# Residual stream kept token by feature: row-wise norms, turned tiles, token-wise output projections, and other lanes' blocks ahead of the steps of x's norms

## The reference, cut to what matters

```python
h = rms_norm(x, g_pre)            # over the 1024 features of a token
x = x + rms_norm(mix_or_ffn(h), g_post)
```

```python
(silu(h @ w_gate) * (h @ w_up)) @ w_down
```

## Time and profile before

| | |
|---|---|
| median of 3 runs | 2696.52 us (2694.02 to 2698.24) |
| the profiled execution | 2697.63 us |
| its span, first to last instruction | 2695.9 us |
| TensorE (PE) busy | 2507.8 us, 93% |
| VectorE (DVE) busy | 1706.4 us, 63% |
| ScalarE (ACT) busy | 1242.5 us, 46% |
| granted TensorE clock, mean | 0.969 |
| DMA read | 471.48 MB, 175 GB/s |

### The profile page before, as it was taken

The page is one execution under the profiler, slowest core; times in us unless marked ns, Lnnn a source line. Parts: engine busy times, 40 slices in busy tenths (PEclk is TensorE's granted clock), DMA queues, the critical chain, the costliest instruction groups (busy, mean ns, idle before and its releaser), DMA issues.

```text
span 2695.9 us, 48269 instructions
## 1 busy us (share of the span) xinstructions
PE 2507.8 (93%) x20500; PEld 2368.0 (88%) x20500; DVE 1706.4 (63%) x2804; ACT 1242.5 (46%) x1687; POOL 1.2 (0%) x6
## 2 busy tenths in 40 slices
PE   5799997899999999999998999999999999787998
PEld 5689996788998898999797999999999999766997
DVE  5565565456766656566777667577575558656655
ACT  4443352344545445455455544464444345444443
POOL 0000000000000000000000000000000000000000
PEclk9899998899999999999898999999999999898999
DMA  5456655623555665544362344455545555363453
GB/s 213 180 194 255 240 198 223 246 104 119 188 186 206 232 252 188 176 152 159 118 202 80 122 157 172 170 189 174 187 171 177 185 173 187 118 235 125 172 180 117
DMA packets 71588, 480.09 MB, mean 178 GB/s; under 512 B 8784, under 2 KB 9296, under 8 KB 17744
## 3 DMA queue, kind: packets, MB, share of 16 engines
q1 hardware_dynamic: 66240, 468.74, 48.9%
q10 hardware_dynamic: 5136, 8.28, 1.0%
HBM read 471.48 MB, written 1.05 MB: 175 GB/s over the span
## 4 chain that ended last, share of the span: by engine, by line
PE 75%; DVE 12%; ACT 6%; DMA 4%; issue 3%; ACTq 0%; DVEq 0%
PE bank L265 65%; ACT whi L224 3%; DMA raw<-w_main 2%; DVE wlo L244 2%; PE bank L302 2%; PE bank L1163 2%; DVE wlo L231 2%; PE bank L1045 1%; DMA raw<-w_down 1%; PE bank L983 1%; DVE HX L685 1%; DVE ARX L734 1%; DVE tmpx L679 1%; PE bank L1033 1%; DMA tmpx<-ARX 0%
## 5 line engine op out<-in xcount | busy, mean ns | idle before, releaser
L265 PE MATMUL bank<-HNX_hi,whi 128*128 128x256 f32 x2872 | 832.9, 291 | 46.0 <-DVE wlo L244 19.1
L224 ACT ACTIVATE whi<-raw 128x2048 fp32r<-128x2048 f32 (+1 forms) x378 | 705.6, 1868 | 337.5 <-PE bank L265 154.5
L265 PE MATMUL bank<-HNX_hi,wlo 128*128 128x256 f32 x2872 | 819.4, 286 | 0.0
L231 DVE TENSOR_TENSOR wlo<-raw,whi 128x1024 fp32r<-128x1024 f32 (+1 forms) x378 | 453.4, 1199 | 561.6 <-ACT whi L224 560.8
L265 PE MATMUL bank<-HNX_lo,whi 128*128 128x256 f32 x2872 | 804.8, 286 | 0.0
L265 PEld LDWEIGHTS bank<-HNX_hi,whi 128*128 128x128 f32 x2872 | 560.5, 195 | 71.3 <-issue 39.4
L265 PEld LDWEIGHTS bank<-HNX_hi,wlo 128*128 128x128 f32 x2872 | 561.1, 195 | 0.0
L265 PEld LDWEIGHTS bank<-HNX_lo,whi 128*128 128x128 f32 x2872 | 552.0, 195 | 0.7 <-issue 0.5
L244 DVE TENSOR_TENSOR wlo<-raw,whi 128x1024 fp32r<-128x1024 f32 (+1 forms) x378 | 451.2, 1194 | 0.0
L265 PE MATMUL bank<-HNC_hi,whi 128*128 128x256 f32 x1280 | 372.8, 291 | 8.4 <-DVE tmpc L496 5.3
L265 PE MATMUL bank<-HNC_lo,whi 128*128 128x256 f32 x1280 | 365.1, 285 | 0.0
(11 more groups left out here) (363 smaller groups left out, 2923.7 us busy)
## 6 DMA issues: line engine op xcount, KB each, us to landing
raw<-w_main SPq DMA_DIRECT2D x270, 1024.0 KB, 4.8
raw<-w_ada SPq DMA_DIRECT2D x72, 1024.0 KB, 4.8
raw<-w_down SPq DMA_DIRECT2D x72, 1024.0 KB, 4.9
raw<-w_down SPq DMA_DIRECT2D x36, 768.0 KB, 4.2
raw<-w_cmp SPq DMA_DIRECT2D x4, 1024.0 KB, 5.7
tmpx<-ARX ACTq DMA_DIRECT2D x18, 128.0 KB, 5.3
tmpx<-ARX ACTq DMA_DIRECT2D x32, 64.0 KB, 4.8
HX<-x_in SPq DMA_DIRECT2D x2, 512.0 KB, 5.8
```

Of the source, the lines that this page charges most:

```text
L224: NS.activation(WHI[q % HIS][:, 0:size], RAW[m % SLOTS][:, 0:size], ACT.Copy).then_inc(sems["w_hi"], 1)
L231: NV.tensor_tensor(WLO[m % SLOTS][:, 0:half], RAW[m % SLOTS][:, 0:half], WHI[q % HIS][:, 0:half].bitcast(fp32), SUB)
L265: return NT.matmul(dst, (WHI[ordinal[n] % HIS], WLO[n % SLOTS])[w][:, k * 2 * P + col:k * 2 * P + col + P], x[xp][:, kx, :], start=start, ...
```

## The change

The residual of each lane lies as `[128 tokens, 2, 1024 features]`. Output projections (`mix_out`, the down part of `ffn`) use `token_tiles`, which gives 128 tokens by 512 features per bank; x's 12 down blocks stay 12, the first of each half smaller. A sum of squares is then the accumulator of a ScalarE square along the row (`square_rows`), a root and a reciprocal are one column, the post gain is a row held in all partitions (`GROW`, fetched by `grow` through the POOL queue; for the second stack from a scratch tensor that `gate_row` writes), and the residual update is one operation per 512 features. The second norm squares the new residual itself. The normed rows are turned back to feature by token by 16 transposes through TensorE (four groups, banks 4, 2, 3, 4 for x, 6 and 7 for c), and gain and shift go with the copies out of the bank. x yields L 2.2 before the steps and 0.5 ahead of the turns, nothing in between; c has `pause` between its steps. The inputs, the output and the weights' order in memory follow. Sums, diagonals and `put_out` go.

```diff
-CHUNKS = ((0, 8), (8, 16), (16, 22))
-SHORT_FIRST = ((0, 6), (6, 14), (14, 22))
+CHUNKS = ((0, 4, 8), (8, 12, 16), (16, 20, 22))
+SHORT_FIRST = (0, 2, 6, 10, 14, 18, 22)
...
-        HX, HC = sb("HX", [P, KD, T]), sb("HC", [P, KD, T])
+        HX, HC = sb("HX", [P, 2, D]), sb("HC", [P, 2, D])
...
+                 (BANK[2], BANK[3], BANK[0], BANK[1]), (BANK[0], BANK[1]), (BANK[4], BANK[2], BANK[3], BANK[4]), False, False)
+        C = Lane("c", 1, HC, HNC, by_rows(YC_ALL), GC, TMPC, STATC, GROWC, 64,
+                 (BANK[6], BANK[7], BANK[6], BANK[7]), (BANK[6], BANK[7]), (BANK[6], BANK[7], BANK[6], BANK[7]), True, True)
...
+            def square_rows(S, src, at, junk, *ready):
+                sq = up(f"{S.tag}_sq")
+                if on(act, *ready):
+                    NS.activation(junk, src, ACT.Square, accum_out=S.STAT[:, at:at + 1]).then_inc(sq.sem, 1)
...
+            def gained(S, h, m, src, sq):
+                ev, cols = up(f"{S.tag}_gained"), slice(h * 2 * T, (h + 1) * 2 * T)
+                if on(dve, sq, grown[S.tag]):
+                    NV.tensor_tensor(S.Y[:, m, cols], src, S.GROW[:, cols], MUL).then_inc(ev.sem, 1)
...
+            def put_first(S, m, src, ready):
+                sq = square_rows(S, src, 2 * m, spare(S, m, 0), ready)
+                return half_mean(S, 2 * m, 4 + m, sq), gained(S, 0, m, src, sq)
...
+            def grow(S, src, *ready):
+                landed_ = up(f"{S.tag}_grow", 16)
+                if on(pool, *ready, now(f"{S.tag}_gained") if count[f"{S.tag}_gained"] else None):
+                    pool.dma_start(S.GROW[:, :] if len(src.shape) == 2 else S.GROW[:, :].rearrange("p (r q) -> p r q", r=4), src).then_inc(landed_.sem, 16)
+                grown[S.tag] = landed_
...
+            def mix_out(S, name, ready):
+                parts, firsts = {}, {}
+                for h in range(2):
+                    banks, tile = S.tiles[2 * h:2 * h + 2], up(f"{S.tag}_tile")
+                    for c in range(2):
+                        yield ("D",)
+                        n = take(S.tag, "w_main", MAIN[name] + 2 * h + c)
+                        if c == 0:
+                            settle(S)
+                            on(pe, *ready, *(free.get(b.name) for b in banks))
+                        yield from token_tiles(S, n, banks, S.HN, [(k, 4 * c + k) for k in range(4)], c == 0, c == 1, None, tile if c else None, h == 1 and c == 1)
+                    if h:
+                        tail[S.tag] = [(parts[m], firsts[m], banks[m], banks[m][:, :], done(n) if m else tile) for m in range(2)]
+                        continue
+                    def job(n=n, banks=banks, tile=tile):
+                        for m in range(2):
+                            parts[m], firsts[m] = put_first(S, m, banks[m][:, :], done(n) if m else tile)
+                            free[banks[m].name] = firsts[m]
+                    after(S, job)
...
+                        for h in range(2):
+                            banks, tile = S.tiles[2 * h:2 * h + 2], up(f"{t}_tile")
+                            for cc, (k0, k1) in enumerate(zip(SHORT_FIRST, SHORT_FIRST[1:])):
                                 yield ("D",)
-                                n = take(t, "w_down", (4 * which + mp, k0 * 2 * P), (k1 - k0) * 2 * P)
+                                n = take(t, "w_down", (2 * which + h, k0 * W_TOK), (k1 - k0) * W_TOK)
                                 if cc == 0:
                                     on(pe, *(free.get(b.name) for b in banks))
                                 ks = [(k - k0, k) for k in range(k0, k1)]
-                                waits = {k: [lo_marks[k // 2]] for k in range(k0, k1) if k % 2 == 0} if mp == 0 else None
-                                tile = up(f"{t}_tile") if cc == 2 else None
-                                yield from two_tiles(S, n, [b[:, 0:T] for b in banks], S.G, ks, cc == 0, cc == 2, waits, tile, 2, mp == 3 and cc == 2)
+                                waits = {k: [lo_marks[k // 2]] for k in range(k0, k1) if k % 2 == 0} if h == 0 else None
+                                yield from token_tiles(S, n, banks, S.G, ks, cc == 0, k1 == KF, waits, tile if k1 == KF else None, h == 1 and k1 == KF)
...
+            def pause(S, us):
+                if S.lag:
+                    yield ("L", us)
+            def root_of(S, at, bias, dst, *ready):
+                root, inv = up(f"{S.tag}_root"), up(f"{S.tag}_rstd")
+                if on(act, *ready):
+                    NS.activation(S.STAT[:, dst:dst + 1], S.STAT[:, at:at + 1], ACT.Sqrt, bias=bias, scale=1.0 / D).then_inc(root.sem, 1)
+                return root, inv
...
+            def norm(S, post, pre, mod=None, ready=None, opening=False, then=None):
+                t, ST = S.tag, S.STAT
+                HALF = [slice(h * 2 * T, (h + 1) * 2 * T) for h in range(2)]
+                back, roots = {}, {}
                 if post:
+                    last = tail.pop(t)
                     if t == "x":
                         table_of(ACT.Sqrt)
+                    yield ("L", 3.0 if S.lag else 2.2)
+                    sqs = []
+                    for m, (part, first, bank, src, done_) in enumerate(last):
+                        sqs.append(square_rows(S, src, 2 * m + 1, spare(S, m, 1), done_))
+                        if not S.lag:
+                            roots[m] = root_of(S, 2 * m + 1, ST[:, 4 + m:5 + m], 6 + m, sqs[m], part)
+                    yield from pause(S, 2.0)
+                    evs = []
+                    for m, (part, first, bank, src, done_) in enumerate(last):
+                        if S.lag:
+                            roots[m] = root_of(S, 2 * m + 1, ST[:, 4 + m:5 + m], 6 + m, sqs[m], part)
+                        evs.append(gained(S, 1, m, src, sqs[m]))
+                        if bank is not None:
+                            free[bank.name] = evs[m]
+                    yield from pause(S, 2.0)
+                    for m, (part, first, bank, src, done_) in enumerate(last):
+                        inv = inverse(S, 6 + m, *roots[m])
+                        for h in range(2):
+                            re = up(f"{t}_resid")
+                            if on(dve, inv, (first, evs[m])[h]):
+                                NV.scalar_tensor_tensor(S.H[:, m, HALF[h]], S.Y[:, m, HALF[h]], ST[:, 6 + m:7 + m], S.H[:, m, HALF[h]], MUL, ADD)\
+                                    .then_inc(re.sem, 1)
+                            back[m, h] = re
                 if not pre:
+                    return back
+                yield from pause(S, 3.0)
+                if post:
+                    means = {}
+                    for m in range(2):
+                        sq0, sq1 = (square_rows(S, S.H[:, m, HALF[h]], 8 + 2 * m + h, S.Y[:, m, HALF[h]], back[m, h]) for h in range(2))
+                        means[m] = half_mean(S, 8 + 2 * m, 12 + m, sq0), sq1
+                    yield from pause(S, 2.0)
+                    for m in range(2):
+                        roots[m] = root_of(S, 9 + 2 * m, ST[:, 12 + m:13 + m], 14 + m, *means[m])
...
                 if then is not None:
                     table_of(then)
                 if opening:
                     splits(-1, most=1)
+                yield from pause(S, 2.0)
+                scaled = {}
+                for m in range(2):
+                    inv = inverse(S, 14 + m, *roots[m])
+                    for h in range(2):
+                        scaled[m, h] = sc = up(f"{t}_scaled")
+                        if on(dve, inv):
+                            NV.tensor_scalar(S.Y[:, m, HALF[h]], S.H[:, m, HALF[h]], ST[:, 14 + m:15 + m], None, MUL).then_inc(sc.sem, 1)
+                yield ("L", 2.0 if S.lag or not post else 0.5)
+                if mod:
+                    mod = (yield from await_rows(*mod)) if S.lag else need(*mod)
+                    if act:
+                        for x in mod:
+                            act.wait_ge(*x)
+                    if dve:
+                        for x in mod:
+                            dve.wait_ge(*x)
                 gain, shift = pre
+                his, los = [], []
+                for kk in range(4):
+                    bank, turned = S.turns[kk], up(f"{t}_turned")
+                    if on(pe, free.get(bank.name)):
+                        for m in range(2):
+                            pe.wait_ge(*scaled[m, kk // 2])
+                            for j in range(2):
+                                k = 2 * kk + j
+                                mm = NT.transpose(bank[:, j * T + m * P:j * T + (m + 1) * P], S.Y[:, m, k * P:(k + 1) * P], ident)
+                        mm.then_inc(turned.sem, 1)
+                    if opening and kk == 1:
                         splits(-1)
...
+                    if shift is None:
+                        for k, src, tmp in parts:
+                            hi = up(f"{t}_hn_hi")
+                            if on(act, turned):
```

(34 more changed lines are left out.)

553 lines of the change are left out of this document (195 added, 358 removed).

## The result

The changed kernel takes **2707.5 us** (median of 11 executions, 2700.9 to 2710.0) against 2697.8 for the kernel before (11 executions): a ratio of 1.0037, interval 1.0028 to 1.0046. It is slower by 0.37%, about 10 us, where 2668 was forecast: outside the forecast's own range of 2653 to 2690, inside the wider one of 2638 to 2710 that took in the rivals. The profiled execution has a span of 2704.7 us, 8.8 more than before.

What follows compares the result with a forecast made beforehand. TensorE, busy 93% of the span, and its stops inside x's norms were taken as the bound. Terms -34.5 + 6 - 39 + 23 + 13 + 3 = -28.5 gave 2668 us; own range 2653 to 2690, with rivals 2638 to 2710.

Steps and rivals of the forecast that it cites:

- Wide products: Down and output projections: 119 groups of 24 wide products save 0.29 us each, -34.5 us.
- The rivals on their price: Wide products no faster here: 2702 us, or 2695 by the skill's fixed cost; chance 0.04.
- Turns: 16 transposes per norm replace totals and spreads: +6 us in ten covered norms, bounds +3 to +10.
- Bare norms: Norms of x at ev_out, ffn2, ffn4, ga_out, plus opening and end: shorter chain, -39 us, from -25 to -50.
- The middle of the chain: Exposed norm of x, first square to first turn: 7.8 us within a chain of 9.7 us.
- the split that "stays": Opening: weight splits stay while reductions over x and the spread go, -6 us.
- Covered norms: ffn0, od_out, ffn1, da_out, ffn3: 29.7 us idle against 11.7, plus 5 of low clock, +23 us.
- norms are bared: Rival: chain waits for splits, lane c's activation work and late DMA; 13 us idle per covered norm, 2715 us; chance 0.18.
- Lane c: Early arrival at turns in its norms +5, waits for banks 6 and 7 at three places +8: +13 us.
- a sign of being wrong: TensorE waiting for an evacuation of bank 6 or 7, listed among what would show the forecast wrong.
- ends nearly where it did: Lane c: half blocks move but its pauses shrink, so its end hardly moves; two ga_in blocks fall behind x's.
- the rest: Short block first in each down half, weight slots turning over faster beside ADA: +3 us; gain and gate rows 0.

Runs made afterwards that it cites:

- e4: Changed kernel with each 512 wide token-wise product made as two products 256 wide; 2740.7 us, ratio 1.0165.
- e7: Changed kernel with each of the 16 turns of a norm made twice into the same place; 2712.7 us, ratio 1.0057.
- e9: Changed kernel with the opening's split of the first weight block behind the first norm's reciprocals and scalings; 2705.3 us, ratio 1.0020.
- e3: Changed kernel with lane c's down projections releasing both banks first and the next half waiting for bank 7 only before its second half; 2698.2 us.
- e12: Changed kernel with five spread half blocks, early bank release, opening's split behind scalings, lane c's evacuation right behind its half block; 2656.5 us.

## Why the forecast failed, step by step

*Wide products: right.* Forecast -34.5; the spacing is 227 ns, and e4 puts them at 32, within its uncertainty. The rivals on their price are out. The estimate from the Trainium skill, page "TensorE: Matmul & The Clock Gate", section "Wait — 56ns, not 53.3ns?", a saving of 7 us, is out with them.

*Turns: price right, term too high.* Four cost 0.44 to 0.50 us at the full clock (0.44 forecast), and by e7 the 240 turns are 26 us of work. But the work at full clock, less 33 for the products (e4's 35.9 for 129 groups, taken for 119), fell by 5 where +6 stood in ten norms alone. By difference, what went away with the totals and spreads was worth 31 us, where 1.3 a norm gives 21 in 16 norms. The 275 ns of the Trainium skill, same page, section "Part 4: PE-mode transpose", are not borne out for a stream: 0.125 us each in the row of 2349.28.

*Bare norms: the first step that failed, -39 against -21.6.* ffn4 (-6.5, measured -5.8) and the end (-6.5, -5.9) were right; ffn2 (-8) gave 1.2, ev_out (-9.5) 6.7, the opening (-6) 1.2, ga_out (-2.5) 0.8. The middle of the chain was right: 7.1 to 8.5 us from the first square to the first turn, where the terms give 7.8. It was mis-sized at both its ends. At its start the first square comes 0.6 to 3.2 us after the last product, where none was priced. In ev_out (3.2) a table load and a split stand ahead of it, as in od_out above. ga_out shows a table load of 1.28 us that the sum left out:

```profile
2494.79 1.28 ACT L604 ACT_TABLE_LOAD   x1
2496.09 0.20 ACT L604 ACTIVATE SMALL<-VEC 128x1 f32<-128x1 f32 x1
2496.19 0.58 ACT L397 ACTIVATE ARX<-bank 128x512 f32<-128x512 f32 x1
...
2503.98 0.66 PE L702 MATMUL bank<-VEC,ARX 128*128 128x128 f32 x2 [8.70 <-DVE ARX L683]
2504.88 3.25 PE L702 MATMUL bank<-VEC,ARX 128*128 128x128 f32 x14 [0.24 <-DVE ARX L683]
...
2507.78 0.56 PE L264 MATMUL bank<-HNX_hi,whi 128*128 128x256 f32 x1
```

At its end the first turn is 3.8 us ahead of the first product, priced at 1.9: the first four turns wait for the third scaling, and run at 1.2 GHz. In ffn2 a softmax of lane c stood on VectorE ahead of x's pieces. In the opening the split that "stays" stood ahead of the reciprocals, as e9 shows.

*Covered norms: idle time right, clock wrong.* 29.7 us of idle time were forecast, 28.9 measured. The low clock was priced at 5 and cost 14. The mechanism was seen (splits ahead of the first step). Lane c's activation work, which waits for its block on TensorE and holds the first square longest (ffn3, 7.0 us), stood in the rival alone. The rival "norms are bared" asked for 13 us of idle time each; it is not what happened.

*Lane c: the step that failed most, +13 against +36.2.* The wait for banks 6 and 7 was named, also as a sign of being wrong, and put only into back-to-back stretches, the attentions, at 2.7 us each. The dense stages stood in the sum at nothing, and they lost 29.5 us more. There the wait falls where both lanes alternate: of the four stops of 2.4 to 5.6 us that e3 aimed at, three end with an evacuation and one with a split, and three have low clock behind them. Evacuations and splits share a queue in order. The earlier release of the banks takes 12 of the 29.5 us away (e3), and with spread pauses and the evacuation handed out at once 22 are gone (e12). That lane c "ends nearly where it did" was wrong as well: 101 us instead of 83 in ga's attention. Most of these 18 us are its own work moved there; the loss in that stretch grew by 3.

By terms: the bare norms missed by 17 us, the covered ones by 9 and lane c by 23; the work gained 9 more than forecast and the rest cost 3 less. Together 37 us, the distance from -28.5 to +8.8. Not settled: how lane c's share divides between its banks (9 us of the time in e3), late splits and its lag.

## What to carry to other kernels

When two streams of work share in-order engines, a pause is worth what stands next to it in every queue. Cover taken in a heap ahead of a chain puts its own evacuation and activation ahead of the chain's first step, and in a heap behind it waits for the chain's last; alternate block and step, and count in each queue what each step waits for. The amount comes first, though: spread over the steps here, three half blocks gained 4 us and five gained 29. After a change of form, recount how much the second lane gets done under cover, for what is not taken there comes back bare at the next place that needs it.

## What the runs showed of the hardware

Added TensorE work can be nearly free: 240 more turns, 26 us of work, cost 5 us, since the idle time fell by 8 us and the time at 1.2 GHz from 211 to 173. The Trainium skill, page "TensorE: Matmul & The Clock Gate", section "Part 4: PE-mode transpose", says that such turns do not count as busy for the clock; the granted clock of 0.94 against 0.83 in the same stretch speaks against it here. The rows call the turns MATMUL and do not say whether they use the mode that the page means.

A change of activation table costs 1.28 us on ScalarE in a norm's chain, and the next instruction starts 0.02 us behind it. The Trainium skill, page "ScalarE: Activation LUTs", section "What ACT_TABLE_LOAD costs", adds about 1.4 us of draining; the rows at 2494.79 and 2496.09 show none.
